# Two transformer blocks on one core: the delta rule in chunks of 64 tokens, low parts of the weights placed by a planner, and a head in column halves

## The reference

```python
CHUNK = 64
gc = jnp.cumsum(chunks(g), axis=-1)                      # within a chunk
decay = jnp.exp(jnp.where(causal, gc[..., :, None] - gc[..., None, :], -jnp.inf))
a_mat = jnp.where(strict, bc[..., :, None] * kk * decay, 0.0) + jnp.eye(CHUNK)
sol = lax.linalg.triangular_solve(a_mat, rhs, left_side=True, lower=True)
u, w = sol[..., :dv], sol[..., dv:]
def step(state, xs):                                     # one chunk
    v_new = u_n - w_n @ state
    o = (q_n * exp(g_n)) @ state + attn_n @ v_new
    state = state * exp(gl_n) + kt_n.T @ v_new
```

## Time and profile before

| | before |
|---|---|
| median of three runs | 1189.45 us (1188.62 to 1190.49) |
| the profiled execution's own time | 1190.16 us |
| its span, first to last instruction | 1188.4 us |
| TensorE busy in it | 1152.7 us (97%) |
| VectorE, ScalarE, GpSimd busy | 815.0, 619.2, 84.4 us |
| DMA | 193.95 MB, 163 GB/s over the span |
| mean granted TensorE clock | 0.993 of 2.4 GHz |

### The profile page before, as it was taken

The page is one execution under the profiler, slowest core; times in us unless marked ns, Lnnn a source line. Parts: engine busy times, 40 slices in busy tenths (PEclk is TensorE's granted clock), DMA queues, the critical chain, the costliest instruction groups (busy, mean ns, idle before and its releaser), DMA issues.

```text
span 1188.4 us, 16775 instructions
## 1 busy us (share of the span) xinstructions
PE 1152.7 (97%) x6763; PEld 1005.9 (85%) x6763; DVE 815.0 (69%) x881; ACT 619.2 (52%) x800; POOL 84.4 (7%) x117
## 2 busy tenths in 40 slices
PE   6999999999999899999999999999999998999997
PEld 6887888888988789999888888888776887888886
DVE  5877656865778767877647777646876757777743
ACT  6656345434768655565536444436455547444442
POOL 8001200300000000000000000002700000000000
PEclk9999999999999999999999999999999999999999
DMA  8544323333655436555655566565633523765550
GB/s 254 164 159 156 107 72 105 113 121 124 212 187 168 142 98 204 181 192 184 210 191 177 178 192 198 180 205 174 212 130 118 188 82 125 214 198 186 183 207 36
DMA packets 144420, 193.95 MB, mean 163 GB/s; under 512 B 6168, under 2 KB 121240, under 8 KB 144344
## 3 DMA queue, kind: packets, MB, share of 16 engines
q1 hardware_dynamic: 143144, 188.43, 49.0%
q0 software_dynamic: 1200, 4.46, 1.1%
HBM read 191.82 MB, written 1.05 MB: 162 GB/s over the span
## 4 chain that ended last, share of the span: by engine, by line
PE 86%; DVE 8%; ACT 3%; issue 2%; DMA 1%; SPq 0%; DVEq 0%; ACTq 0%
PE banks L1279 23%; PE banks L1313 20%; PE banks L1261 14%; PE banks L1282 11%; PE banks L1298 5%; DVE wlo L1867 3%; PE banks L1289 2%; PE banks L1536 1%; ACT whi L1596 1%; PE banks L1372 1%; PE banks L1415 1%; PE banks L1327 1%; PE banks L1424 1%; PE banks L1422 1%; DMA raw<-in_w_in 1%
## 5 line engine op out<-in xcount | busy, mean ns | idle before, releaser
L1867 DVE TENSOR_TENSOR wlo<-raw,whi 128x2048 fp32r<-128x2048 f32 x178 | 408.0, 2294 | 176.4 <-ACT whi L1596 176.3
L1596 ACT ACTIVATE whi<-raw 128x2048 fp32r<-128x2048 f32 x178 | 339.4, 1910 | 173.7 <-PE banks L1313 85.0
L1279 PE MATMUL banks<-xhl,whi 128*128 128x512 f32 x1232 | 397.7, 404 | 2.8 <-DVE gv_ L1959 1.0
L1282 PEld LDWEIGHTS banks<-xhl,wlo 128*128 128x128 f32 x1232 | 232.2, 188 | 54.8
L1282 PE MATMUL banks<-xhl,wlo 128*128 128x256 f32 x1232 | 243.3, 279 | 0.0
L1279 PEld LDWEIGHTS banks<-xhl,whi 128*128 128x128 f32 x1232 | 189.8, 190 | 10.5 <-issue 5.4
L1261 PE MATMUL banks<-xhl,whi 128*128 128x256 f32 x912 | 166.7, 286 | 0.0
L1261 PEld LDWEIGHTS banks<-xhl,whi 128*128 128x128 f32 x912 | 143.8, 194 | 0.4 <-DVE xhl L1894 0.2
L1261 PE MATMUL banks<-xhl,wlo 128*128 128x256 f32 x456 | 129.9, 285 | 0.0
L1313 PE MATMUL banks<-wlo,hh 128*128 128x512 f32 x264 | 102.8, 389 | 0.0
L1313 PE MATMUL banks<-whi,hh 128*128 128x512 f32 x264 | 102.8, 389 | 0.0
(11 more groups left out here) (367 smaller groups left out, 1539.0 us busy)
## 6 DMA issues: line engine op xcount, KB each, us to landing
raw<-in_w_in SPq DMA_DIRECT2D x40, 1024.0 KB, 5.3
raw<-in_w_up SPq DMA_DIRECT2D x22, 1024.0 KB, 5.1
raw<-in_ffn_w_gate SPq DMA_DIRECT2D x22, 1024.0 KB, 5.4
raw<-in_ffn_w_up SPq DMA_DIRECT2D x22, 1024.0 KB, 5.3
raw<-in_ffn_w_down SPq DMA_DIRECT2D x22, 1024.0 KB, 5.0
raw<-in_w_down SPq DMA_DIRECT2D x11, 1024.0 KB, 5.0
raw<-in_w_out SPq DMA_DIRECT2D x8, 1024.0 KB, 5.1
raw<-in_xa_wkv SPq DMA_DIRECT2D x8, 1024.0 KB, 5.4
```

The source lines that it names most:

```text
L1279: pe.matmul(bank(b[m]), wh[:, k, m * P:(m + 1) * P], both[:, k, :, :].rearrange("p a t -> p (a t)"), start=(k == 0), stop=(k == KD - 1), s ...
L1282: ins = pe.matmul(bank(b[m])[:, 0:T], wl[:, k, m * P:(m + 1) * P], Xh[:, k, :], start=False, stop=(k == KD - 1), skip_group_check=True)
L1596: act.activation(whi[c % RING][:, :], raw[c % RING][:, :], ACT.Copy).then_inc(act_done, 1)
L1867: dve.tensor_tensor(wlo[c % RING][:, :], raw[c % RING][:, :], whi[c % RING][:, :], ALU.subtract).then_inc(dve_done, 1)
```

## The change

- The delta rule takes chunks of 64 tokens (CH = 64). The inverse needs block sizes up to 64, so one of the seven levels goes, and the masks `gda` and `gdat` are cut at the 64-token border. The recurrence has two steps for each token block, each with half the tokens: `r_ws` with 64 columns of weights, `r_o` with pairs of matmuls of 64 moving columns (one of the pair with 128 rows, the other with 64; the order within the pair alternates over the heads), and the update of the state with 64 rows.
- `lo c` is no longer placed with `hi c`. It is pending, and placed at the next quarter at which its high part is planned to be ready (`low_part`), at the latest at the end of `mm c-2`. Behind FFN chunks it comes at the chunk's start, behind the steps carried over from the chunk before.
- In `hook`, links that are functions (norm turns) are placed behind the others that are ready.
- A `hook` is placed between `pl_h` and `pl_l`.
- The head: all masks but the levels come first on GpSimd; TensorE does 20 transposes of the identity before the parameters and 14 behind them (`warm`); chunk 0 is split in column halves: `hi 0 0` on ScalarE, `lo 0 0` on VectorE, then, between the turns of the norm, `hi 0 1` on ScalarE and its low part on GpSimd (`low_right`).

```diff
-CH = 128
-LEVELS = 7
+CH = 64
+WARM = (20, 14)
+LATE = 0.3
@@ Plan costs
-... "r_o": 2.6, "r_oc": 0.63, "r_s": 1.1,
+... "r_o": 1.8, "r_oc": 0.35, "r_s": 1.1,
@@ build_plan
+    def low_part(force=False):
+        if pending and (force or not side or pl.ended["hi", pending[0]] <= max(pl.clock["dve"], pl.clock["pe"]) + LATE):
+            pl.add("dve", "lo", pending.pop())
     def hook(force=False):
...
-                if i < len(link_):
+                if i < len(link_) and not callable(link_[i]):
                     finished[id(chain)] = place(link_[i], finished.get(id(chain), 0.0))
+        for link_ in links:
+            if callable(link_[0]):
+                place(link_[0])
         side[:] = [chain for chain in side if chain]
+        low_part()
@@ mm(c)
-        if early:
-            split(c + LEAD)
+        if early and c + LEAD < n:
+            pl.add("act", "hi", c + LEAD)
+            pending.append(c + LEAD)
...
+        low_part()
         quarter(c, 0)
...
         pl.add("pe", "mm", c, 1)
+        low_part(True)
@@ gdn(t)
-        for l in range(1, LEVELS):
+        for l in range(1, 6):
...
-        c += [[("pe", "r_ws", t), ("dve", "r_vn", t)],
-              [("pe", "r_o", t), ("act", "r_oc", t), ("dve", "r_s", t)]]
+        for j in range(2):
+            c += [[("pe", "r_ws", t, j), ("dve", "r_vn", t, j)],
+                  [("pe", "r_o", t, j), ("act", "r_oc", t, j), ("dve", "r_s", t, j)]]
@@ the head
     pl.add("pool", "consts")
+    pl.add("pool", "consts2")
+    pl.add("pe", "warm", 0)
     pl.add("pe", "params")
     pl.add("dve", "params_c")
+    pl.add("pe", "warm", 1)
     norm_scale("norm_mix")
-    split(0)
-    norm_turn("norm_mix", 4)
+    pl.add("act", "hi", 0, 0)
+    pl.add("dve", "lo", 0, 0)
+    norm_turn("norm_mix", 4, beside={2: [("act", "hi", 0, 1), ("pool", "low_right")]})
     split(1)
-    pl.add("pool", "consts2")
+    pl.add("pool", "levels")
@@ the second block's mix
-    mm(c + 2, mid=[("pe", "pl_mm"), ("act", "pl_h"), ("dve", "pl_l")])
+    mm(c + 2, mid=[("pe", "pl_mm"), ("act", "pl_h"), hook, ("dve", "pl_l")])
@@ TensorE
+            def warm(i):
+                pe.wait_ge(pool_done, at("consts"))
+                for _ in range(WARM[i]):
+                    ins = pe.transpose(bank(2)[:, 0:P], ident[:, :], ident[:, :])
+                ins.then_inc(pe_done, 1)
-            def r_ws(t):
+            def r_ws(t, j):
+                r = slice(j * CH, (j + 1) * CH)
...
-                    ins = pe.matmul(bank(4)[:, h * P:(h + 1) * P], gU[:, h, :], gS[:, h, :], start=True, stop=True)
+                    ins = pe.matmul(bank(4)[r, h * P:(h + 1) * P], gU[:, h, r], gS[:, h, :], start=True, stop=True)
-            def r_o(t):
+            def r_o(t, j):
...
-                    pe.matmul(o, gS[:, h, :], gq_[:, h, s], start=True, stop=False)
-                    pe.matmul(o, gMs0[:, h, :], gAT[:, h, :], start=False, stop=True)
+                    pair_ = ((gS[:, h, :], gq_[:, h, s]), (gMs0[r, h, :], gAT[r, h, r]))
+                    for i, (a, v) in enumerate(pair_ if h % 2 == 0 else pair_[::-1]):
+                        pe.matmul(o, a, v, start=(i == 0), stop=(i == 1))
                 for h in range(NH):
-                    ins = pe.matmul(bank(4)[:, h * P:(h + 1) * P], gKt[:, h, :], gMs0[:, h, :], start=True, stop=True)
+                    ins = pe.matmul(bank(4)[:, h * P:(h + 1) * P], gKt[r, h, :], gMs0[r, h, :], start=True, stop=True)
@@ GpSimd
+            def low_right():
+                pool.wait_ge(act_done, at("hi", 0, 1))
+                pool.tensor_tensor(columns(wlo, 0, 1), columns(raw, 0, 1), columns(whi, 0, 1), ALU.subtract).then_inc(pool_done, 1)
```

More of the change, by code:

```diff
@@ L75 @@
          "g_vb": 1.0, "l_mask": 1.7, "l_u": 0.9, "l_uc": 0.63, "l_x": 1.8, "l_upd": 1.3, "g_uw": 1.8, "g_u": 0.6, "g_w": 0.63,
-         "g_bc": 0.9, "g_egc": 0.63, "g_qg": 0.6, "r_ws": 0.9, "r_vn": 0.6, "r_o": 2.6, "r_oc": 0.63, "r_s": 1.1,
+         "g_bc": 0.9, "g_egc": 0.63, "g_qg": 0.6, "r_ws": 0.9, "r_vn": 0.6, "r_o": 1.8, "r_oc": 0.35, "r_s": 1.1,
          ("sc", "fox"): 1.3, ("sm", "fox"): 1.25, ("ex", "fox"): 0.9, ("pn", "fox"): 0.85, ("pt", "fox"): 0.67,
@@ L89, with low @@
           "hn_sum": "hn_sq"}
+def low(c, part=1):
+    return ("lo", c) if c else (("lo", 0, 0), ("low_right",))[part]
 class Plan:
@@ L551, in norm_turn @@
             pl.add("pe", "nt", name, j)
+            for step in beside.get(j, ()):
+                pl.add(*step)
             pl.add("act", "nh", name, j)
@@ L897, in two_blocks_kernel, with columns @@
         dist = cmask
-        def level(l):
-            return lev[:, l, :] if l < LEVELS - 1 else lev_last[:, :]
+        def columns(tiles, c, part):
+            tile = tiles[c % RING][:, :]
+            if part is None:
+                return tile
+            return tile.rearrange("p (k n) -> p k n", n=width(chunks[c]))[:, :, part * P:(part + 1) * P]
         def half_of(h):
@@ L1238, in multiply @@
                 slot, (Xh, Xl), b = c % RING, XHL[ch["x"]], ch["banks"]
+                if 0 in quarters and c == 0:
+                    pe.wait_ge(*((pool_done, at("low_right")) if part else (dve_done, at("lo", 0, 0))))
                 if part == 0 and 0 in quarters:
-                    pe.wait_ge(dve_done, at("lo", c))
+                    if c:
+                        pe.wait_ge(dve_done, at("lo", c))
                     for step in plan.ready[c]:
```

91 lines of the change are left out of this document (53 added, 38 removed).

## The result

| | before | after |
|---|---|---|
| median of 16 runs | 1189.13 us (1186.4 to 1191.13) | 1192.33 us (1189.2 to 1195.41) |
| after / before | | 1.0028 (95%: 1.0019 to 1.0036) |
| the profiled execution's own time, its span | 1190.16, 1188.4 us | 1193.79, 1192.0 us |
| mean granted clock over the runs | 0.9937 (23 runs) | 0.9933 (16 runs) |

The change made the kernel slower by 0.28%, a little over what can be told from no change. I had forecast 1189.2. One later execution of the kernel before took 1631.95 us at a mean granted clock of 0.655; it was in the slow state and is left out of every number here, which compare fast runs with fast runs.

A forecast was written before the change was run, and what follows sets the result against it. TensorE, busy 97% of the span, was taken as the bound. Terms −2.8 − 5.3 + 7.1 + 5.4 − 4.0 − 3.1 + 2.5 summed to −0.2, giving about 1189.2 us median, range 1181.5 to 1195.

The forecast's parts named there:

- Head, −2.8: Head: chunk 0 in halves starts weight matmuls 2.0 us earlier, added transposes may bring full pace; 2.8 us saved.
- rival E: Head: TensorE stays at half pace because transposes don't raise the clock; +1.3 us, 1190.5 us, chance 0.05.
- Level, −5.3: Delta rule: one level of the inverse less saves 2.67 us of TensorE per token block, 5.3 us for both.
- recurrence, +7.1: Delta rule: the recurrence runs twice per token block, each matmul pass at full price; 7.1 us added.
- Rival B: Recurrence: passes of 64 columns cost half and changes of the array's shape nothing; −9.0 us, 1180.2 us, chance 0.20.
- Changes of shape, +5.4: Recurrence: alternating 128-row and 64-row matmuls costs 1.34 us per half recurrence, four of them; 5.4 us added.
- Waits between 63 and 300, −4.0: Delta rule's stretch: with low parts placed later, TensorE's 6.1 us of waits fall to about 2; 4 us saved.
- First memory attention, −3.1: First memory attention: waits fall from 3.2 to 1.75 us (−1.4), half the slow-clock part goes (−1.7).
- rival C: Clock comes back: no half-clock part stays in the memory attention, mix hides its 2.8 us; 1184.7 us, chance 0.13.
- Pooled mix, +2.5: Pooled mix: later `pl_l` delays matmuls by 2.8 us, older waits shrink, possible clock fall adds 0.8; 2.5 us added.
- FFNs at nothing: FFNs: low parts behind the activations still end before their chunk needs them; no change in time.
- Rival D: Late low parts: memory attention keeps its slow clock, the mix's clock falls; +4.5 us, 1193.7 us, chance 0.20.

The follow-up runs named there:

- e5: The kernel before with only the new head (masks first, added transposes, chunk 0 in column halves): 1187.77 us.
- e8: The changed kernel with 1 + 1 transposes of the identity in place of 20 + 14 in the head: 1192.91 us.
- e2: The changed kernel with the recurrence's pairs and state product in the array's full shape, only the state's update at 64 rows: 1187.14 us.
- e9: The changed kernel with the delta rule in chunks of 128 tokens again, all updates of X included: 1183.43 us.
- e7: The changed kernel with the two matmuls of each pair in the same order for every head, so more shape changes: 1195.04 us.
- e1: The changed kernel with the delta rule in chunks of 128 tokens again, but one update of X per token block left out: 1184.21 us.
- e4: The changed kernel without the hook between `pl_h` and `pl_l`: 1195.82 us.
- e3: The changed kernel with each low part placed right behind its high part again: 1192.10 us.
- e6: The changed kernel with the delta rule in chunks of 128 tokens and each low part right behind its high part: 1186.52 us.
- e10: As e9, but low parts late only up to chunk 35, later ones with their high parts, and no hook before `pl_l`: 1180.80 us.

## Why the prediction was wrong

I forecast no measurable change, 1189.2; it was 1192.33, inside the range, and slower, to which I gave 0.28. The sum had +0.7 us of work and waits and −0.9 of clock; measured were +2.6 and +0.5 over the runs, +1.9 and +1.7 between the two traces. Two steps failed: the recurrence was summed without the clock, and behind the delta rule the late low parts were taken to save work and waits (−1.4 in the memory attention, nothing in the FFNs) where both stretches got longer by 1 us. The traces' misses of the opposite sign, in the changes of shape and in the clock of the memory attention, are why the sum came as near as it did. Step by step:

- **Head, −2.8: right.** −2.87 in the traces, −2.2 to −2.5 in e5. The right low part on GpSimd took 2.38 us (2.5 estimated), chunk 0's first matmul came at 12.67 (12.8). The transposes' part was sized too high, 1.3 us against 0.3 to 0.7 in e8. That they bring full pace is shown (0.125 us a transpose at 10.24 us with them, 0.23 without), which doesn't agree with the Trainium skill's rule that I cited, by which work in transpose mode doesn't count; rival E fell.
- **Level, −5.3, and recurrence, +7.1: right.** A pass with 64 moving columns takes 0.11 us (e2), and there are twice as many. The level was not measured by itself; with the changes of shape as measured the three terms make 5.5, and after is 5.6 us over e9 at full clock. Rival B fell. Its other end, +3.6, was wrongly added up besides: half the price for the pairs alone makes +3.6, with `r_ws` at half too it is +1.8.
- **Changes of shape, +5.4: mis-sized.** A half recurrence takes 1.02 + 2.39 + 1.08 = 4.49 us, 0.93 above 3.56, where I had 1.34: 3.7 us in all. A change costs 0.14 to 0.16 us, not 0.2 (e2, e7).
- **The clock of the recurrence, at nothing: a step that failed.** I let the clock follow from waits alone, and so only in the memory attention and the mix. In the recurrence the runs show 2.5 us of clock between after and e1 and 2.6 between after and e2 (3.4 in the traces). TensorE had no gap ahead of those stretches; what it did was small matmuls that change shape. That this is what brings the clock down is borne out by the clocks and traces of twelve kernels (under e7), and is still a matter of odds, as e4 shows.
- **Waits between 63 and 300, −4.0: right in size (−3.8), wrong in reason.** I put it down to the late low parts. e3 shows these waits gone without them, e6 against e9 that at 128 tokens the late placement is what removes them. In the changed kernel it therefore had nothing left to gain there, only its price elsewhere: e3 is 2.3 us faster at full clock.
- **First memory attention, −3.1: −2.3, near by chance; the second step that failed.** The clock gave 3.4 us where I had 1.7: it was at 1.00 throughout, the first half of rival C. In none but one (e7) of the seven traces with late low parts there (after, e1, e2, e4, e7, e8, e9) did it fall, and it fell in all five with early ones (before, e3, e5, e6, e10). I had also misread: the clock fell at 411.6, behind the first wait, and the second lay inside the slow part. Work and waits were to give 1.4 us and cost 1.1. The wait at the transpose went, but the one at the down projection grew to 2.22 us (1.75 forecast), one of 0.9 that I had overlooked came, and TensorE is busy longer with the same number of matmuls, 102.76 against 105.05 less the 3.4 of clock, or 1.1 us:

```profile
343.22:451.48 108.26, 105.05 (x584) 89.19 (x585) 78.48 (x93) 70.56 (x114) 1.51 (x4) 0.97 0.50 163
344.76:450.68 105.92, 102.76 (x584) 87.40 (x585) 78.03 (x93) 70.61 (x114) 1.51 (x4) 1.00 0.51 168
```

The first is before, the second after. The 1.1 us are not explained. The wait of 0.9 is: two low parts in a row on VectorE hold up a head norm.

```profile
386.57 4.48 DVE L1925 TENSOR_TENSOR wlo<-raw,whi 128x2048 fp32r<-128x2048 f32 x2
...
391.09 0.75 DVE L2026 SCALAR_TENSOR_TENSOR mq_<-mq_,pcol,xv_ 128x512 f32<-128x512 f32 x1
...
391.99 1.10 PE L1421 MATMUL banks<-xv_,ones 128*128 128x512 f32 x2 [0.90 <-DVE mq_ L2026]
```

The wait at the transpose is gone in e6 and e3 too, with early low parts, and stays in e5. What those two share with after is that norm turns stand behind the other links; no run took that edit alone.

- **Pooled mix, +2.5: +3.4.** `pl_l` ended at 878.94 + 1.66 = 880.60, 5.3 us later than before (3.6 forecast). The new waits were 0.34 and 1.30 us, not 0.75 and 2.05; and of the old ones 0.63 went and 1.28 became 1.49, so all waits there went from 3.2 to 4.4; the clock took 1.7 in this trace where I had 0.8.
- **FFNs at nothing: wrong at one place.** At 460.3 a chunk waits 0.54 us for its low part, behind another one (4.49 us for the two); from start to start it costs 0.7 of the stretch's 1.0. e3 has no such wait.

Rival D, slower by late low parts and the clock, was nearest in time, but of its places only the mix, where the clock fell, came true. Open is some 1.6 us of work: with the sizes above the sum at full clock comes to about 1.0 us, measured were 2.6, give or take about 0.7. Of the rest the traces place 1.1 us in the memory attention, and say no cause. Open too is why the mean clock is lower with early low parts (0.9916 in e3 against 0.9933). The fall in the memory attention, which every trace with early low parts has, will be part of it; one profile each cannot say how much.

## What to carry to other kernels

- A level or an instruction saved is to be weighed against the passes that it adds: half as many moving columns saved nothing here, 0.11 us a pass either way with 128 columns of weights, and matmuls that alternate between 64 and 128 rows cost 0.14 to 0.16 us at each change and, on top, clock.
- On one engine that is busy 97%, the mean granted clock of many runs belongs beside the time: 0.001 of it was 1.03 us, and a profile shows only one draw.
- Two edits that remove the same wait don't add up. Placing ready work first paid in one stage and cost in others; decide it by stage.
- A sum can come near by errors that cancel: forecast work and clock apart for each stage, and compare each with its own measurement.

## What the runs showed of the hardware

- The granted clock fell to 0.50 (1.2 GHz) for 3.4 us with TensorE busy without a gap ahead, right behind fp32 matmuls that alternate between 128 and 64 rows; in e2, with the same count at 128 rows, it stayed at 1.00 there. It isn't certain to fall: in e4 the same matmuls at the same places, 0.08 us later, had 1.00.
- A change between 128 and 64 rows cost 0.14 to 0.16 us (1.82, 2.39 and 2.72 us for the same 16 passes with one, five and seven changes); a pass of 64 moving columns took 0.11 us, as one of 128 does.
- Behind the added transposes everything in the head ran at full pace, the norm's 14 transposes at 10.24 us included. In e8 full pace came at 14.9 us, with the same turns of the norm as before the change, where it came at 19.2. That difference I had not expected and have not explained.
- A subtraction of 128x1024 on GpSimd took 2.38 us, the same on VectorE 1.23.
